# Gated delta rule and attention gates: the first gate projection placed, tile by tile, inside the chain of the two chunks

## The reference, cut to what matters

```python
def step(state, inp):
    qd, ke, u_c, w_c, qk_c, gl = inp
    v_new = u_c - jnp.einsum('bhcd,bhde->bhce', w_c, state)
    o = jnp.einsum('bhcd,bhde->bhce', qd, state) + jnp.einsum('bhij,bhje->bhie', qk_c, v_new)
    state = state * gl[..., None, None] + jnp.einsum('bhcd,bhce->bhde', ke, v_new)
    return state, o
...
        mix = jax.nn.sigmoid(gate_dn) * (o_dn @ w_proj_dn[l]) + jax.nn.sigmoid(gate_nsa) * (o_ns @ w_proj_nsa[l])
        x = x + mix @ w_out[l]
```

## Time and profile before

| | us |
|---|---|
| median of 3 runs | 989.91 (989.89 to 991.35) |
| the profiled execution | 992.16 |
| its span in the trace | 990.3 |
| TensorE busy with matmuls | 930.4 (94%) |
| VectorE busy | 630.7 (64%) |
| ScalarE busy | 464.1 (47%) |
| granted TensorE clock, mean | 0.981 |

### The profile page before, as it was taken

One profiled execution on the slowest core, in us unless ns is written; L12 is line 12 of the kernel. 1 busy time (PEld: TensorE's weight loads), 2 busy tenths in 40 slices (PEclk: granted clock), 3 DMA queues, 4 the chain that ended last, 5 costly groups with the idle time before them and its releaser, 6 DMA issues. The chain is left out here.

```text
span 990.3 us, 17478 instructions
## 1 busy us (share of the span) xinstructions
PE 930.4 (94%) x6842; PEld 823.3 (83%) x6842; DVE 630.7 (64%) x1341; ACT 464.1 (47%) x924; POOL 155.8 (16%) x111
## 2 busy tenths in 40 slices
PE   4999989999999979599999999898999999999998
PEld 2996778999999969588988898897888789999986
DVE  4557566656556676777897987625756666444543
ACT  5454555545344455236434674253444455445441
POOL 2000000000000005100975314000000013223321
PEclk9998999999999989799999999999999999999999
DMA  8540234465566433536441201202555546555551
GB/s 302 174 143 1 88 126 128 150 212 174 173 192 213 152 109 128 203 110 217 153 147 66 65 13 44 87 3 79 172 176 170 170 134 225 184 182 170 176 186 43
DMA packets 38678, 139.61 MB, mean 141 GB/s; under 512 B 4330, under 2 KB 4586, under 8 KB 38596
## 3 DMA queue, kind: packets, MB, share of 16 engines
q1 hardware_dynamic: 37184, 134.17, 40.8%
q10 hardware_dynamic: 884, 2.49, 0.8%
q0 software_dynamic: 528, 1.84, 0.7%
HBM read 137.39 MB, written 1.08 MB: 140 GB/s over the span
## 5 line engine op out<-in xcount | busy, mean ns | idle before, releaser
L1774 DVE TENSOR_TENSOR parts<-raw,parts 128x1024 fp32r<-128x1024 f32 (+1 forms) x227 | 288.1, 1307 | 151.6 <-ACT parts L1272 149.8
L1272 ACT ACTIVATE parts<-raw 128x1024 fp32r<-128x1024 f32 (+1 forms) x227 | 229.9, 1050 | 130.1 <-PE psum L521 101.0
L519 PE MATMUL psum<-hT,parts 128*128 128x256 f32 (+1 forms) x928 | 264.0, 285 | 2.3 <-DVE hT L1791 2.0
L520 PE MATMUL psum<-hT,parts 128*128 128x256 f32 (+1 forms) x928 | 262.7, 283 | 0.0
L521 PE MATMUL psum<-hT,parts 128*128 128x256 f32 (+1 forms) x928 | 261.1, 281 | 0.0
L519 PEld LDWEIGHTS psum<-hT,parts 128*128 128x128 f32 x928 | 175.0, 189 | 5.7 <-DVE hT L1791 2.9
L521 PEld LDWEIGHTS psum<-hT,parts 128*128 128x128 f32 x928 | 176.2, 190 | 0.0
L520 PEld LDWEIGHTS psum<-hT,parts 128*128 128x128 f32 x928 | 175.2, 189 | 0.6
L519 PE MATMUL psum<-parts,arena_r 128*128 128x512 f32 x344 | 137.5, 400 | 3.6 <-issue 3.0
L521 PE MATMUL psum<-parts,arena_r 128*128 128x512 f32 x344 | 136.3, 396 | 0.0
L520 PE MATMUL psum<-parts,arena_r 128*128 128x512 f32 x344 | 136.3, 396 | 0.0
(11 more groups left out here) (316 smaller groups left out, 1183.3 us busy)
## 6 DMA issues: line engine op xcount, KB each, us to landing
raw<-weights SPq DMA_DIRECT2D x247, 512.0 KB, 4.1
raw<-weights SPq DMA_DIRECT2D x4, 384.0 KB, 7.3
X<-x SPq DMA_DIRECT2D x2, 512.0 KB, 6.2
out<-X SPq DMA_DIRECT2D x2, 512.0 KB, 2.6
arena<-lines POOLq DMA_DIRECT2D x1, 768.0 KB, 9.9
cbuf<-consts ACTq DMA_DIRECT2D x1, 561.0 KB, 5.2
arena<-lines POOLq DMA_DIRECT2D x1, 544.0 KB, 7.7
arena<-params ACTq DMA_DIRECT2D x1, 512.0 KB, 8.8
```

The costliest lines, as they stand in the source:

```text
L519: mm(ps, a, c, start=start, stop=False)
L520: mm(ps, a, d, start=False, stop=False)
L1272: signal(A(split_slot(name)[0], whole_piece, ACT.Copy), "first_parts")
L1774: signal(V_.tensor_tensor(second, whole_piece, first.bitcast(F32), ALU.subtract), "split_vector")
```

## The change

TensorE: the first of the four gate projections, `gn0`, is taken apart by token tile. Tile 0 (24 matmuls) runs after `vn_0_1`, before the state `s1_q` is made. In the second chunk both `ks_q` jobs now run first, then tile 1 of `gn0` (24 matmuls), then `vn_1_0` and `vn_1_1`. While tile 0's job and those up to `ks_1` are closed, the splitting ahead is cut at `gn1.1`. The pieces of `gn0` are kept for the second pass (`again=True`). After the chain `gn1`, `gd0` and `gd1` remain, as before.

ScalarE: both sigmoids of `gn0` are evicted behind the two copies of the carried state and ahead of the copies of `vn_1_q`. They go to other places in memory, as `gn0` and `gn1` now run while parts of the old target are still in use.

VectorE: only the address from which the gates are read later.

```diff
+        gates_nsa = [half.rearrange("p (t n) -> p t n", t=TT) for half in (dn["DT"][:, 1024:2048], nsa["cv"][:, 4096:5120])]
...
             for t in range(TT):
+                if t == 1:
+                    for q in range(2):
+                        freed(pe, f"s1_{q}")
+                        heads_job(f"ks_{q}", q, lambda h: cv[:, 0, h, P:SEQ], lambda h: S1[:, h, :])
+                    limit[0] = None
+                    token_products("gn0", [("gn0_1", tiles2[1])], hT)
                 for q in range(2):
                     freed(pe, f"y{LEVELS - 1}_{2 * t + q}")
                     if t == 1:
-                        freed(pe, f"s1_{q}")
-                        heads_job(f"ks_{q}", q, lambda h: cv[:, 0, h, P:SEQ], lambda h: S1[:, h, :])
                         pe.wait_ge(sem("vb1"), q + 1)
                     heads_job(f"vn_{t}_{q}", q, lambda h: Y4[:, t, h, :], lambda h: Vb[:, t, h, :])
+                if t == 0:
+                    limit[0] = "gn1.1"
+                    token_products("gn0", [("gn0_0", tiles2[0])], hT, again=True)
...
-            for tag in ("gn", "gd"):
-                for n in range(2):
-                    two_tokens(f"{tag}{n}", f"{tag}{n}")
+            for unit in ("gn1", "gd0", "gd1"):
+                two_tokens(unit, unit)
...
+            def gate_out(n, t):
+
+                name = f"gn{n}_{t}"
+                full(act, name)
+                release(A(gates_nsa[n][:, t, :], bank_of(name), ACT.Sigmoid), name)
+
             for q in range(2):
                 full(act, f"s1_{q}")
                 ins = A(S1[:, GH * q:GH * q + GH, :], bank_of(f"s1_{q}"), ACT.Copy)
                 release(ins, f"s1_{q}")
+            for t in range(TT):
+                gate_out(0, t)
             for q in range(2):
                 full(act, f"vn_1_{q}")
                 full(act, f"o_0_{q}")
                 release(A(VN[:, 0, GH * q:GH * q + GH, :], bank_of(f"vn_1_{q}"), ACT.Copy), f"vn_1_{q}")
 
-            sgs = nsa["cv"][:, 4096:6144].rearrange("p (t n) -> p t n", t=TT)
-            for n in range(2):
-                for t in range(TT):
-                    name = f"gn{n}_{t}"
-                    full(act, name)
-                    if n == 0 and t == 0:
-                        full(act, "os_1")
-                    release(A(sgs[:, t, 512 * n:512 * n + 512], bank_of(name), ACT.Sigmoid), name)
+            full(act, "os_1")
+            for t in range(TT):
+                gate_out(1, t)
```

More of the change, by code:

```diff
@@ L2436, in attention_share @@
                     full(dve, name)
-                    release(V_.tensor_tensor(mix[:, t, s_], bank_of(name), sgs[:, t, s_], ALU.mult), name)
+                    release(V_.tensor_tensor(mix[:, t, s_], bank_of(name), gates_nsa[n][:, t, :], ALU.mult), name)
             attention_share(0)
```

## The result

The change makes the kernel slower by a little: the ratio to the kernel before is 1.0017, with a 95% interval of 1.0010 to 1.0023, which is +1.7 us (1.0 to 2.3) on a median of 991.7 us for the kernel before in 22 runs (992.9 us after, 22 runs). The three runs of the kernel before that were known ahead, with their median of 989.91, lay low among these 22 (one is 991.35, two are 989.9). The profiled execution after has a span of 992.3 us, 2.0 more than before, and a mean granted clock of 0.978 (0.981 before).

What follows compares the result with a forecast made beforehand. TensorE was taken to bound the kernel; -3.9 us for filled holes, 4.1 to 4.7 for a new wait, 1.4 to 2.5 for the clock and 0 to 0.2 for ScalarE gave +2.5, 992.4 us from 989.91, range 990.1 to 993.9.

Steps and rivals of the forecast that it cites:

- The holes: TensorE's three waits between groups of small matmuls over the two chunks, 4.1 us by starts; filling them nets -3.9 us.
- Nothing else late in the chain: Pieces of gn1 split in time at no cost, ScalarE's sigmoids and table load hidden, banks free: 0, at most 0.2 us.
- rival 3: ScalarE's sigmoid, table load or a split holds up vn_1_0, losing 0.1 to 1.9 us; +3.5 to +5.4 us; chance 0.08.
- The cover: Before gd0, half of TensorE's 22.4 us of work now precedes the chain's end; a new wait of 4.1 to 4.7 us.
- my two ends: Pause on VectorE between its last eviction, L2406, and what follows: 0.04 or 0.67 us, both kept.
- The clock: Behind the new wait at gd0, TensorE's granted clock falls to half and slows 512-column matmuls: 1.4 to 2.5 us, middle 1.9.
- Rival 1: Same stall before gd0, but the clock stays at 1.00 or falls only briefly: +0.2 to +1.1 us; chance 0.12.
- The rule that the prediction quoted: A wait between two bursts of matmuls puts the array back to half rate; the loss is the throttled time times one half.
- The sum: Whole kernel: -3.9 + (4.1 to 4.7) + (1.4 to 2.5) + (0 to 0.2) = +1.6 to +3.5 us, middle +2.5.
- Rival 4: Nothing moves, what the holes held is lost elsewhere, with no stall over 3 us: 989.9 us; chance 0.03.
- Rival 2: Holes pay in full if VectorE splits gd0.0's second half before the norm, so TensorE never waits: 986.0 us; chance 0.06.

## Why the prediction was right, and where it was off

*The holes.* Forecast -3.9 us, measured -4.3 by starts (the kernel with the splits in the norm's midst, 34.94 against 39.28). The 48 records in a row take 5.3 us between starts where I reckoned 5.45.

*Nothing else late in the chain.* Right: no idle time stands in it after the change. The pieces of `gn1` were split from 668.95 and from 680.87 on, the last one done at 683.5 (forecast 684.1), `vn_1_0` was copied in time, and no further wait appeared; rival 3 is out. (Its sum was off besides: a loss of 0.1 to 1.9 us on top of +1.6 to +3.5 begins at +1.7, not at +3.5.) The sigmoids ran at 677.55 and 683.89 (forecast 677.9 and 684.6).

*The cover.* Right in place, cause and size: 4.1 to 4.7 us forecast, 4.23 measured by the idle time and 4.4 by starts (from 700.29 to 704.68), ended by the split behind the norm. It is shown from four sides: it moves on when one more piece is split first (2.66), it shrinks with two (1.01), it is gone with three split in time, and it appears in the kernel before when the norm is made longer (4.03). `gd0` started 0.1 us later than before, where I had 0.25 to 0.85. Two things made the difference. The pause of the earlier trace rows behind VectorE's last eviction was 0.13 us here (690.73 to 690.86), near the lower of my two ends. And that eviction ended 25.44 us behind the chain's start where I had 25.77, mostly because the groups of 48 records ran faster than I reckoned.

*The clock.* Right in kind; 1.4 to 2.5 us forecast, 2.3 in the profiled execution, in which the granted clock was 0.77 from 700 to 705 and 0.55 from 705 to 710. Filling the wait with matmuls separates it from the wait and takes away 1.8 us by the two ratios (1.0017 to 0.9999). Rival 1, the wait without the clock, is out for the profiled execution, and by the two ratios for the executions taken together. One premise was weaker than I took it for: the wait of 2.99 us, which I counted as followed by half rate, is followed by full rate in five of the ten traces (the last section has the numbers). The rule that the prediction quoted from the Trainium skill, TensorE: Matmul & The Clock Gate, section "HAM oscillation — how this bites in real kernels", agrees with these traces behind the waits of 2.19 to 4.23 us: the matmuls of the changed kernel ran slow for 4.8 us, from 704.68 to 709.5, of which one half is 2.4, and 2.3 were lost. Behind the waits of 1.01 and 1.51 us there was no half rate, and behind that of 2.99 us none in five traces; where the rule and these traces differ, the traces decide.

*The sum.* The forecast was +2.5 us with +1.6 to +3.5 as its own range; measured +1.7 (1.0 to 2.3). The direction was right and the middle 0.8 us too high, which matters for one number: I gave 0.64 to slower by more than 0.2%, and the measured 0.17% (0.10 to 0.23) lies on the other side of that line. That the time came out at 992.9, so near to the 992.4 forecast, is in part luck: the median I started from, 989.91, was 1.8 us below that of the 22 runs, and the two medians lie 1.2 us apart where I had 2.5; the two errors nearly cancel. The step that was a little too large is the start of `gd0` (0.1 in place of 0.25 to 0.85). Over many executions the clock's part seems nearer 1.8 than 2.3, but the intervals are too wide to settle that. Rival 4, no stall of over 3 us, is out with the wait of 4.23.

*Rival 2, the gain in full*, is what the change gives once `gd0.0` to `gd0.2` are split in time: 3.9 us were put on it, 4.7 (3.4 to 5.9) came. The program's order on VectorE was all that stood in the way, and that edit by itself is worth nothing (-0.2 us, interval -1.0 to +0.7).

## What to carry to other kernels

Work that is moved into a hole is taken away from where it stood, and there it may have been covering something: before filling a hole, add up what the other engines do in the time that the moved work now covers, and see by how much they were ahead (here 0.6 us, with 11.2 us of cover taken away). A long run of instructions on an engine that also prepares weights should be broken where the next consumer needs a piece; look for that when a filled hole brings nothing. A wait is charged twice if TensorE's clock falls behind it, so two holes of 1.5 us at full clock (3.0 us) can be cheaper than one of 2.2 behind which 1.6 more are lost.

## What the runs showed of the hardware

The granted clock did not always fall inside a wait. In the changed kernel it did (0.77 from 700 to 705). But after 4.03 us of idle TensorE ran three matmuls at full rate before they slowed at 708.54, and after 2.66 us the clock was still 1.00 when it resumed, up to 707.00. So an engine that has already resumed can still be slowed; the likely reason is the gap just behind it, since in the kernel before, without that gap, the clock is 1.00 from 693.70 to 727.00. In this stage waits of 1.01 and 1.51 us left the clock at 1.00; those of 2.19, 2.66, 4.03 and 4.23 each brought the half rate (1.2 and not 2.4 GHz), for a loss between 1.6 and 2.3 us in the twelve matmuls behind them. The length of the wait did not set the size: 4.03 us cost 1.6, 4.23 cost 2.3.

The length of a wait did not settle whether the clock fell either. All ten kernels run the same work up to the chain, and each has the wait of 2.99 us of the earlier trace rows (2.99 to 3.01). In five of the ten traces the granted clock from 120 to 130 is 0.79 to 0.84, in the other five it is 1.00, and the first matmul behind the wait takes 0.47 or 0.48 us there and not 0.76 or 0.77. In the kernel before, behind a wait of only 1.07 us at 517.5, the clock was 0.83 from 518 to 519 and 0.50 from 519 to 522; all ten have that wait too, and the clock from 510 to 530 is below 1.00 in seven. So a fall in one profiled execution does not show that every execution has it. Such falls are likely a part of why executions of one kernel differ by some 4 us (989.59 to 993.96 for the kernel before), but no run here isolates that.
